# Gates 2 to 5 of an input projection with three of four weight chunks in halves

## The chip, the cores and the metric

The kernel runs on one core of a Trainium2 chip. The metric is the device time of one execution in microseconds. The engines are named as in the profile: PE is TensorE, ACT is ScalarE, DVE is VectorE, POOL is GpSimd, SP is SyncE, which issues the transfers.

## The reference, cut to what matters

Two blocks of two layers each work on 256 tokens of width 1024, in float32. The change lies in the first block, in the mixer of each of its two layers:

```python
h = rmsnorm(x, norm_mix[l])
(u_ssm, q_lat, kv_lat, k_rope, hg_q, hg_f, hg_i, hg_g, gate_logits) = jnp.split(h @ w_in[l], split_at, axis=-1)
...
gates = jax.nn.sigmoid(gate_logits.astype(jnp.float32)).reshape(bsz, s, N_BRANCH, D_MODEL)
merged = (gates[:, :, 0] * y_ssm + gates[:, :, 1] * y_mla + gates[:, :, 2] * y_hg)
x = x + merged @ w_out[l]
```

`gate_logits` is h (256 x 1024) times 3072 columns of `w_in`. The kernel makes it in six products of 512 columns, called gates 0 to 5 here. Between them stands work of the third branch (`hgrn2_mixer`): its attention with decay is built of eight nested levels (distances 64, 32, ... 1, and across the two halves), each of which needs differences and exponentials of summed logarithms, two products by q and k, and small matrix products.

## The kernel before

**Two ways to multiply.** `product` (lines 395 to 402) multiplies float32 operands directly (line 398), or operands that were split into a high and a low half in the type fp32r (line 400): high by high, high by low, low by high, three matmuls. The first is whole, the second in halves. The low half of a value is the value less its high half.

**A gate.** `token_out(("gate", l, n), ...)` runs `token_steps` (line 408): 1024 rows of weights come in four chunks of 256 rows by 512 columns (0.5 MB). Activations are the stationary operand. Of the four chunks the first and the third are whole (`low=None`), the second and fourth are in halves (`halves=mix_half`) and marked "both". The halves of the matching column tiles 2, 3, 6 and 7 of h lie in HTL, made once in each layer by POOL (`halves_of`, line 1345, called in line 1378).

**Buffers and order.** Raw chunks go round four slots of W (`RSLOTS`), the halves of weights round three slots of WH and WL (`HSLOTS`). SP issues the loads in the order of chunks, each when its slot is free: a whole chunk's slot when PE has used it, a split chunk's slot when its low half is made (`chunk_release`). A WH/WL slot is free when PE has used it (`split_release`). A "both" chunk is split by POOL alone (`both_parts`, line 1322). For the marks "dve" and "pool", ACT makes the high half (`split_to`, line 1459, the copy is recorded under line 1450) and DVE or POOL the low half (`low_parts`, line 1152). Each engine does its share in its own instruction order.

**When ACT splits.** Each eviction on ACT goes through `full` (line 1474), which first makes every high half up to `ahead(name)` (line 272): up to two splits after the ones of that bank, as long as their raw chunks lie within four of it. So the splits come before the eviction in ACT's queue. Before the change gates hold no ACT splits.

**The order around it.** PE (lines 802 to 812): wait for `mix_halves`, gate 0, gate 1, level 0, gate 2, levels 1 and 2, gate 3, levels 3 and 4, gate 4, levels 5 and 6, gate 5, level 7. In layer 0 `ssm_out(l, 3)`, which makes y(l,3), stands between gates 0 and 1, in layer 1 ahead of gate 0. It reads `bu[1]`, which is a view of OT. POOL (lines 1378 to 1382): halves of column tiles, the splits up to gate 5, halves of UT, the splits of the next product. ACT (lines 1792 to 1805): gate 0, a logarithm, gate 1, and for n = 2 to 5 the exponentials of levels 2n−3 and 2n−2 and then gate n (a sigmoid); at n = 4 also a gelu. DVE (lines 2480 to 2486): for each level i the difference (line 2432, waits for the exponentials of level i−1), the taking of level i−2 out of its banks (line 2451), and the two products (lines 2444 and 2445, wait for the exponentials of level i), which set `level_ready` for PE; after levels 3 and 5 also some rotary work.

Of the kernel before, what the change touches and what calls it, by code (L numbers as in the profile page):

```python
# [30 lines left out]
KT = DM // P  # L31
# [35 lines left out]
def build(nc, T, out):  # L67

    with ExitStack() as ctx:
# [14 lines left out]
        HTF = nc.alloc_sbuf_tensor_at("HTF", [P, KT, S], F32, offset=ht_at)  # L84
# [112 lines left out]
        mix_half = (HTL[:, 0:4, :], HTL[:, 4:8, :])  # L197
        glu_half = (OTR[:, 0:2, :], OTR[:, 2:4, :])
        half_slot = lambda k: 2 * (k // 4) + k % 2
        oML = OT[:, 4:8, :]  # L200
# [130 lines left out]
        def _(pe):  # L331
# [75 lines left out]

            def token_steps(tag, wname, l, act, K, c0, cols, low="dve", kstep=2, halves=None):

                ps = [begin(*tag, tt) for tt in range(TT)]  # L410
                for k0 in range(0, K, kstep):
                    src, slot = act, lambda k: k
                    if halves and k0 // kstep % 2:
                        n, w = chunk(tag, rows(wname, l, k0, kstep, c0, cols), kstep, cols, "both")
                        src, slot = halves, half_slot
                    else:
                        n, w = chunk(tag, rows(wname, l, k0, kstep, c0, cols), kstep, cols, low)
# [275 lines left out]
            for l in range(DEPTH):  # L693
# [109 lines left out]
                for n in range(2):  # L803
                    if l == 0 and n == 1:
                        ssm_out(l, 3)
                    token_out(("gate", l, n), "w_in", l, HTF, KT, 3360 + 512 * n, 512, low=None, halves=mix_half)
                level(l, 0)
                for n in range(2, 6):
                    token_out(("gate", l, n), "w_in", l, HTF, KT, 3360 + 512 * n, 512, low=None, halves=mix_half)
                    level(l, 2 * n - 3)  # L810
                    if n < 5:
                        level(l, 2 * n - 2)
# [433 lines left out]
        def _(pool):  # L1246
# [97 lines left out]

            def halves_of(dst, src, *ks):


                pair = lambda t, k: t[:, k:k + 2, :].rearrange("p a b -> p (a b)")
                for k in ks:
                    high, low = pair(dst[0], half_slot(k)), pair(dst[1], half_slot(k))  # L1350
                    link(pool.tensor_copy(high, pair(src, k)))
                    ins = pool.tensor_tensor(low, pair(src, k), high.bitcast(F32), ALU.subtract)
                    if k != ks[-1]:
                        link(ins)
                return ins
# [5 lines left out]
            for l in range(DEPTH):  # L1361
# [14 lines left out]


                signal(halves_of(mix_half, HTF, 2, 6), "mix_halves", l + 1)
                split_to(split_before["gate", l, 5, 1])
                pool.wait_ge(sem["y_ready"], 4 * (l + 1))  # L1380
# [1390 lines left out]
```

How the kernel before makes its waits and increments, by code:

```python
        def wait_full(eng, name, split_to=None):  # L281
            b, n = group[name]
            if split_to:
                split_to(ahead(name))
            eng.wait_ge(sem[f"bank_full{b}"], n)
# [4 lines left out]
        def wait_freed(eng, name):  # L292
            b, n = group[name]
            eng.wait_ge(sem[f"bank_free{b}"], n)
# [41 lines left out]
            def begin(*name):  # L337
                while done["n"] % BANKS in unfinished:
                    done["n"] += 1
                b = done["n"] % BANKS
                done["n"] += 1
                use = uses[b] = uses.get(b, 0) + 1
                unfinished.add(b)
                assert name not in group, name
                group[name] = (b, use)
                if use > 1:
                    pe.wait_ge(sem[f"bank_free{b}"], use - 1)
                return banks[b]
# [10 lines left out]
            def chunk(name, srcs, k, cols, low="dve"):  # L359
                n = len(chunks)
                chunks.append((name, srcs, k, cols))
                if low is None:
                    pe.wait_ge(sem[f"w_full{n % RSLOTS}"], raw_full(n))
                    return n, W[:, n % RSLOTS, 0:k * cols].rearrange("p (k n) -> p k n", k=k)
                m = len(splits)
                splits.append((n, low))
                split_of[n] = m
                s, v = low_done(m)
                pe.wait_ge(sem[s], v)
                chunk_release[n] = (s, v)
                return n, [w[:, m % HSLOTS, 0:k * cols].rearrange("p (k n) -> p k n", k=k) for w in (WH, WL)]
```

## Time and profile before

| what | value |
| --- | --- |
| time, median of 3 runs | 1924.55 us (1923.4 to 1927.83) |
| time of the profiled execution | 1924.34 us |
| its span | 1922.6 us |
| PE busy | 1798.9 us, 94% |
| DVE busy | 1220.9 us, 64% |
| ACT busy | 867.1 us, 45% |
| POOL busy | 314.5 us, 16% |
| chain that ended last, PE's share | 81% (line 400: 47%, line 398: 24%) |

The span is the profiled execution from its first to its last instruction; 1.7 us of its time lie outside. The gates of layer 0 stand at 145 to 235 us, those of layer 1 at 753 to 841 us.

### The profile page before, as it was taken

Reading aid. Unit: us, or ns where it says so; the run is one execution under the profiler, and the core shown is the slowest. Engines: PE = TensorE matmul, PEld = TensorE weight load, DVE = VectorE, ACT = ScalarE, POOL = GpSimd, SP = SyncE. Lnnn points to the kernel's source line nnn. Section 1 sums busy time; section 2 is a strip of 40 time slices with the busy share of each in tenths; the row PEclk is TensorE's granted clock in tenths of the full one; section 3 lists DMA queues with packets and bytes.
Section 4 is the critical chain, followed back from the end, with each engine's and each line's share of the span. In section 5 each row is a group of like instructions: output and inputs, shape, how many; then the busy total and the mean of one; then the engine's idle time right before and its main releaser. Section 6 shows DMA issues by size and latency. Waiting matters only on the chain.

```text
span 1922.6 us, 27084 instructions
## 1 busy us (share of the span) xinstructions
PE 1798.9 (94%) x10038; PEld 1442.9 (75%) x10038; DVE 1220.9 (64%) x1879; ACT 867.1 (45%) x1413; POOL 314.5 (16%) x290
## 2 busy tenths in 40 slices
PE   7999988989999999999888999998899999889998
PEld 6676667669998866667478998656799874669987
DVE  8996755445667892855555566565577746546775
ACT  4224445355444412344455445345555543555553
POOL 5015453020000003457012000101200000130000
PEclk9999999999999999999999999999999999899999
DMA  5444442446565444445154656431455644135554
GB/s 160 131 127 151 133 152 88 143 106 185 159 187 180 122 134 132 138 144 170 37 170 138 188 176 197 143 99 66 121 177 164 197 148 126 56 102 173 167 188 138
DMA packets 192359, 274.61 MB, mean 143 GB/s; under 512 B 25616, under 2 KB 129540, under 8 KB 192228
## 3 DMA queue, kind: packets, MB, share of 16 engines
q1 hardware_dynamic: 191364, 269.86, 45.9%
q0 software_dynamic: 864, 3.02, 0.6%
q8 instruction: 80, 1.31, 0.3%
q14 instruction: 51, 0.42, 0.1%
HBM read 271.78 MB, written 1.05 MB: 142 GB/s over the span
## 4 chain that ended last, share of the span: by engine, by line
PE 81%; DVE 8%; ACT 6%; issue 3%; POOL 1%; DMA 1%; DVEq 0%; ACTq 0%; SPq 0%; POOLq 0%
PE bank L400 47%; PE bank L398 24%; DVE WL L1161 2%; ACT WH L1450 2%; PE bank L671 1%; PE bank L585 1%; POOL WL L1161 1%; PE bank L1021 1%; PE bank L593 1%; PE bank L488 1%; PE bank L871 1%; ACT HTH L1450 1%; DVE bank L2108 1%; DVE NMX L2160 0%; PE bank L1041 0%
## 5 line engine op out<-in xcount | busy, mean ns | idle before, releaser
L1161 DVE TENSOR_TENSOR WL<-W,WH 128x1024 fp32r<-128x1024 f32 x288 | 352.9, 1225 | 230.7 <-ACT WH L1450 222.3
L1450 ACT ACTIVATE WH<-W 128x1024 fp32r<-128x1024 f32 x328 | 347.6, 1060 | 314.3 <-PE bank L400 262.4
L400 PE MATMUL bank<-HTH,WH 128*128 128x256 f32 x1536 | 437.6, 285 | 19.6 <-DVE WL L1161 9.5
L400 PE MATMUL bank<-HTL,WH 128*128 128x256 f32 x1536 | 434.6, 283 | 0.0
L400 PE MATMUL bank<-HTH,WL 128*128 128x256 f32 x1536 | 434.5, 283 | 0.0
L400 PEld LDWEIGHTS bank<-HTH,WH 128*128 128x128 f32 x1536 | 294.6, 192 | 25.2 <-DVE WL L1161 11.7
L400 PEld LDWEIGHTS bank<-HTL,WH 128*128 128x128 f32 x1536 | 294.7, 192 | 0.1
L400 PEld LDWEIGHTS bank<-HTH,WL 128*128 128x128 f32 x1536 | 294.6, 192 | 0.0
L400 PE MATMUL bank<-WH,HTL 128*128 128x512 f32 x672 | 262.9, 409 | 0.0
L400 PE MATMUL bank<-WH,HTH 128*128 128x512 f32 x480 | 193.7, 404 | 15.4 <-POOL WL L1161 9.3
L400 PE MATMUL bank<-WL,HTH 128*128 128x512 f32 x480 | 189.6, 395 | 0.0
L398 PE MATMUL bank<-W,M 128*128 128x512 f32 (+1 forms) x416 | 170.7, 568 | 8.6 <-issue 8.6
L400 PEld LDWEIGHTS bank<-WH,HTL 128*128 128x128 f32 x672 | 127.7, 190 | 32.1 <-issue 5.5
L398 PE MATMUL bank<-W,HTF 128*128 128x512 f32 (+1 forms) x384 | 149.8, 539 | 0.0
L398 PEld LDWEIGHTS bank<-W,M 128*128 128x128 f32 x416 | 82.9, 204 | 82.7 <-issue 78.0
L1161 POOL TENSOR_TENSOR WL<-W,WH 128x1024 fp32r<-128x1024 f32 x40 | 96.9, 2423 | 260.5 <-ACT WH L1450 259.6
L1289 POOL TENSOR_SCALAR QSQ<-QSQ 128x2 f32<-128x2 f32 x9 | 5.1, 570 | 754.3 <-ACT PB L1490 754.3
L400 PEld LDWEIGHTS bank<-WH,HTH 128*128 128x128 f32 x480 | 92.0, 192 | 40.8 <-POOL WL L1161 12.4
L398 PEld LDWEIGHTS bank<-W,HTF 128*128 128x128 f32 x384 | 68.2, 190 | 67.5 <-issue 66.1
L400 PEld LDWEIGHTS bank<-WL,HTH 128*128 128x128 f32 x480 | 91.8, 191 | 18.4
L398 PE MATMUL bank<-HTF,W 128*128 128x256 f32 x448 | 99.6, 381 | 0.6 <-DVE HTF L2383 0.6
L1334 POOL TENSOR_TENSOR WL<-W,WH 128x1024 fp32r<-128x1024 f32 x40 | 97.1, 2428 | 3.2
(405 smaller groups left out, 2506.9 us busy)
## 6 DMA issues: line engine op xcount, KB each, us to landing
W<-in_w_in SPq DMA_DIRECT2D x132, 512.0 KB, 3.7
W<-in_ffn_w_gate_up SPq DMA_DIRECT2D x176, 256.0 KB, 3.4
W<-in_w_up SPq DMA_DIRECT2D x176, 256.0 KB, 3.4
W<-in_ffn_w_down SPq DMA_DIRECT2D x44, 512.0 KB, 4.2
W<-in_w_down SPq DMA_DIRECT2D x44, 512.0 KB, 4.2
W<-in_w_out SPq DMA_DIRECT2D x32, 512.0 KB, 4.3
W<-in_ssm_w_glu SPq DMA_DIRECT2D x16, 512.0 KB, 4.3
W<-in_x_w_kv SPq DMA_DIRECT2D x16, 512.0 KB, 3.4
```

The costliest lines, as they stand in the source:

```text
L398: return pe.matmul(out, at_a(a), at_b(b), start=start, stop=stop, skip_group_check=True)
L400: m = pe.matmul(out, at_a(a[x]), at_b(b[y]), start=(start and i == 0), stop=(stop and i == 2), skip_group_check=True)
L488: m = pe.transpose(ps[:, k * S + tt * P:k * S + tt * P + P], X[:, tt, (2 * j + k) * P:(2 * j + k) * P + P], IDENT[:, :])
L585: ins = pe.matmul(ps[:, tt * S:tt * S + S], qT[:, tt * P:tt * P + P], kT, start=(tt == 0), stop=(tt == TT - 1), skip_group_check=True)
L593: ins = pe.transpose(ps[:, kt * S + tt * P:kt * S + tt * P + P], p_buf(tag, m[1])[:, tt, kt * P:kt * P + P], IDENT[:, :])
L671: m = pe.matmul(ps[:, h * P:h * P + P], ka[:, h, b * P:b * P + P], qa[:, h, b * P:b * P + P], start=(h == 0), stop=(h == HGH - 1), skip_gr ...
L871: m = pe.matmul(ps[64 * (h % 2):64 * (h % 2) + 64, 0:S], vtok[:, kt, h * VD:h * VD + VD], PT[h % 2][:, kt, :], start=(kt == 0), stop=(kt = ...
L1021: pe.matmul(ps[:, tt * S:tt * S + S], qkT[r:r + 64, h // 2, tt * P:tt * P + P], qkT[r:r + 64, 4 + h // 4, :], start=(tt == 0), stop=False, ...
L1161: eng.tensor_tensor(WL[:, m % HSLOTS, 0:width], W[:, n % RSLOTS, 0:width], h, ALU.subtract)\
L1334: signal(pool.tensor_tensor(low, raw, high.bitcast(F32), ALU.subtract), s, v)
L1450: copy = lambda dst, src, scale=1.0: act.activation(dst, src, ACT.Copy, scale=scale)
L2108: signal(tt_(g, g, RB, ALU.mult), "g_scaled", FT * aff_no(tag, l) + f + 1)
```

## The change

A second pair of tiles, `mix_half2`, in the last four slots of OTR (a view of OT), takes the halves of column tiles 4 and 5 of h. POOL makes them once in each layer, after the splits of gate 0 and after y(l,3) is complete in its bank, and signals `mix_halves2`. PE waits for that ahead of gate 2. In gates 2 to 5 the third chunk (k0 = 4) is no longer whole: it is marked "pool", so ACT makes the high half of the weights and POOL the low half, and PE multiplies it in halves. Only the first chunk of these gates stays whole. Gates 0 and 1 are as before.

```diff
+        mix_half2 = (OTR[:, 4:6, :], OTR[:, 6:8, :])
...
-            def token_steps(tag, wname, l, act, K, c0, cols, low="dve", kstep=2, halves=None):
+            def token_steps(tag, wname, l, act, K, c0, cols, low="dve", kstep=2, halves=None, halves2=None):
...
+                    elif halves2 and k0 == 4:
+                        n, w = chunk(tag, rows(wname, l, k0, kstep, c0, cols), kstep, cols, "pool")
+                        src, slot = halves2, lambda k: k - 4
...
                 level(l, 0)
+                pe.wait_ge(sem["mix_halves2"], l + 1)
                 for n in range(2, 6):
-                    token_out(("gate", l, n), "w_in", l, HTF, KT, 3360 + 512 * n, 512, low=None, halves=mix_half)
+                    token_out(("gate", l, n), "w_in", l, HTF, KT, 3360 + 512 * n, 512, low=None, halves=mix_half,
+                              halves2=mix_half2)
...
-            def halves_of(dst, src, *ks):
+            def halves_of(dst, src, *ks, slot=half_slot):
...
-                    high, low = pair(dst[0], half_slot(k)), pair(dst[1], half_slot(k))
+                    high, low = pair(dst[0], slot(k)), pair(dst[1], slot(k))
...
                 signal(halves_of(mix_half, HTF, 2, 6), "mix_halves", l + 1)
+                split_to(split_before["gate", l, 0, 1])
+                wait_full(pool, ("y", l, 3))
+                signal(halves_of(mix_half2, HTF, 4, slot=lambda k: k - 4), "mix_halves2", l + 1)
                 split_to(split_before["gate", l, 5, 1])
```

## Rows read from the trace of the kernel before

**Rows 1.** Windows over both layers' gates, sum row: length, busy by engine, means.

```profile
sum 178.25, PE 178.25 PEld 119.85 DVE 122.66 ACT 74.69 POOL 89.09; mean PE 89.12 PEld 59.93 DVE 61.33 ACT 37.34 POOL 44.55
```

**Rows 2.** Chain that ended last, layer 0, 158 to 220 us: start, length, what.

```profile
159.02 3.63 PE bank L398 x8
162.65 2.76 PE bank L400 x12
...
168.84 2.73 PE bank L400 x12
...
185.70 3.57 PE bank L671 x32
...
201.60 3.57 PE bank L671 x32
...
217.51 3.57 PE bank L671 x32
```

**Rows 3.** The same chain in layer 1.

```profile
771.32 3.43 PE bank L398 x8
...
791.60 3.57 PE bank L671 x32
```

**Rows 4.** Timeline of POOL, layer 0: start, length, line, operation, tiles, count, idle before.

```profile
138.31 0.61 POOL L1351 CAST HTL<-HTF 128x512 fp32r<-128x512 f32 x1
139.00 1.26 POOL L1352 TENSOR_TENSOR HTL<-HTF,HTL 128x512 fp32r<-128x512 f32 x1
...
154.26 1.04 POOL L1332 CAST WH<-W 128x1024 fp32r<-128x1024 f32 x1 [1.30 <-DMA W<-in_w_in]
155.38 2.40 POOL L1334 TENSOR_TENSOR WL<-W,WH 128x1024 fp32r<-128x1024 f32 x1
...
176.13 2.72 POOL L1334 TENSOR_TENSOR WL<-W,WH 128x1024 fp32r<-128x1024 f32 x1
```

**Rows 5.** Timeline of POOL, layer 1, first split of gate 1.

```profile
761.59 1.04 POOL L1332 CAST WH<-W 128x1024 fp32r<-128x1024 f32 x1 [2.74 <-issue]
```

**Rows 6.** Timeline of ACT, layer 0, gate 1 and level 1.

```profile
170.30 1.28 ACT L1551 ACT_TABLE_LOAD   x1 [8.69 <-PE bank L400]
171.59 1.23 ACT L1551 ACTIVATE A<-bank 128x512 f32<-128x512 f32 x2
173.01 1.28 ACT L1780 ACT_TABLE_LOAD   x1 [0.20 <-DVE TB L2432]
174.31 0.63 ACT L1780 ACTIVATE TB<-TB 128x512 f32<-128x512 f32 x1
```

**Rows 7.** Groups of instructions by form, ACT: the high halves of weights.

```profile
L1450 ACT ACTIVATE WH<-W 128x1024 fp32r<-128x1024 f32 x328 | 347.6, 1060 | 314.3 <-PE bank L400 262.4 <-DMA W<-in_w_out 30.3 <-issue 14.3
```

**Rows 8.** Loads of line 1237 at 150 to 180 us, from issue to landing.

```profile
DMA to landing us min/median/max: 3.7/4.3/5.6
```

**Rows 9.** Timeline of DVE, layer 0: products of levels 1, 2, 4 and 6.

```profile
176.63 2.77 DVE L2445 TENSOR_TENSOR TB<-TB,HK 128x512 f32<-128x512 f32 x1
...
183.56 2.77 DVE L2445 TENSOR_TENSOR TB<-TB,HK 128x512 f32<-128x512 f32 x1
...
201.97 0.69 DVE L2445 TENSOR_TENSOR TB<-TB,HK 128x512 f32<-128x512 f32 x1
...
215.19 2.66 DVE L2444 TENSOR_TENSOR TB<-TB,HQ 128x512 f32<-128x512 f32 x1
217.88 0.69 DVE L2445 TENSOR_TENSOR TB<-TB,HK 128x512 f32<-128x512 f32 x1
```

**Rows 10.** Windows around longer idle times of PE: stretch, busy, PEclk, DMA.

```profile
416.40:421.30 4.90, 2.10 (x8) 1.05 (x7) 0.00 (x0) 2.08 (x2) 4.74 (x2) 1.00 0.26 68
...
1290.50:1293.50 3.00, 0.06 (x1) 0.00 (x0) 0.00 (x0) 2.25 (x4) 1.15 (x1) 0.88 0.02 7
1293.50:1296.00 2.50, 2.46 (x6) 2.05 (x7) 1.71 (x8) 1.73 (x3) 1.20 (x1) 0.50 0.00 0
1296.00:1300.00 4.00, 4.00 (x12) 3.18 (x11) 3.12 (x12) 1.07 (x4) 0.00 (x0) 0.55 0.00 0
```

## The prediction

> **What bounds the kernel now.** I read the windows first, then the chain of work that ended last, and then the timelines of POOL, ACT and DVE over the same stretch. The change touches gates 0 to 5 of the two layers. There PE is busy for the whole length of both stretches, 178.25 of 178.25 us [rows 1], so a PE microsecond taken out shortens the run, as long as nothing else is late by then. Per gate the chain shows four chunks and two levels: from level 1 to level 3 it is 201.60 − 185.70 = 15.90 us [rows 2]. A chunk in halves (12 matmuls, line 400) takes 2.73 to 2.76 us, a whole one (8 records, line 398) 3.43 us [rows 2, 3].
>
> Second, how late could the others be? The levels wait for `level_ready`, which ends a chain that DVE and ACT pass to each other: difference, exponentials, two products, next difference. Level 2 is ready at 183.56 + 2.77 = 186.33 and PE wants it at 185.70 + 1.78 = 187.48: 1.15 us to spare. Level 4: 202.66 against 203.38. Level 6: 218.57 against 219.29 [rows 2, 9]. So in layer 0 three levels have 0.7 to 1.15 us of cover. The tables call PE the bound, but this chain runs at nearly its pace.
>
> **Removed.** Four gates in two layers: 8 chunks go from 3.43 to 2.73 us, 0.70 each: −5.6 us, all of it in PE's gap-free stretches. If nothing else moved, 1924.34 − 5.6 = 1918.7.
>
> **Added: the halves of two column tiles, in POOL's queue.** A copy of 0.61 and a subtraction of 1.26 us of 128x512, about 2.0 with gaps [rows 4]. They stand between gate 0's splits and gate 1's, behind a wait for y(l,3). Queued behind them are gate 1's two "both" splits, on which PE waits.
> In layer 0 y(0,3) is made by PE after gate 0 and ends at 159.02, where gate 1 begins [rows 2]. Before, POOL split gate 1's first "both" chunk at 154.26 to 157.78 [rows 4], under gate 0. Now the earliest is 159.2 (wait) + 2.0 + 1.04 + 2.40 + gaps 0.2 = 164.8, and PE wants it at 162.65 [rows 2]: a stall of 2.15 us that nothing covers. It is at least that by the code; with a slow subtraction (DVE works on UT in the same moment; POOL's 1024-wide one goes from 2.40 to 2.72 when DVE interferes [rows 4]) perhaps 3.
> In layer 1 y(1,3) comes before gate 0, and POOL has 2.74 us of idle time ahead of its split at 761.59 [rows 5]. The 2.0 us fit in: nothing. If that cover were gone, POOL would still be done with it well before PE asks at 768.58.
> PE's own new wait for `mix_halves2` before gate 2 costs nothing: it is set some 10 us earlier.
>
> **Added: ScalarE's high half, 8 times 1.06 us [rows 7].** Its place matters more than its length. ACT makes the splits that come up to two after gate n before it takes gate n out of its bank. For gate 1 that is gate 2's third chunk. Its raw slot is free only when PE is done with gate 1's third chunk, which is whole, and a load takes 3.7 to 5.6 us to land, 4.3 in the median [rows 8]. Queued behind that wait on ACT are gate 1's two evictions and the exponentials of level 1, on which DVE and then PE's level 1 and 2 wait.
> Layer 0, hand replay: PE ends gate 1's third chunk at 168.84 + 2.1 = 170.9 [rows 2]; landed 175.1; high done 176.15; table load and evictions 1.28 + 1.23, table load and exponentials 1.28 + 1.29 [rows 6], so level 1's exponentials end at 181.3 instead of 175.6: 5.7 us later, while PE is 2.1 us later.
> For later gates the slot is freed by POOL's split, so the load comes early and ACT's extra 1.06 us lies in its idle time: nothing.
>
> **Added: POOL's low half, 8 times 2.40 us, and what it does to DVE.** POOL's own load is no problem: per gate 2 × 3.5 + 2.4 = 9.4 us of work (with the casts) in 15.2. The price is on DVE. Its product of line 2445 takes 0.69 us at 201.97 [rows 9] but 2.77 at 176.63, where POOL's subtraction ran from 176.13 to 178.85 [rows 4]: DVE ended 0.55 us after POOL. Line 2444 shows it at 215.19 with 2.66. From level 4 ready to level 6 ready [rows 9] is 218.57 − 202.66 = 15.91 us, of which this block is 1.97: unhindered about 13.9. PE's new period is 15.90 − 0.70 = 15.2. So the chain keeps up if POOL blocks it for at most 15.2 − 13.9 = 1.3 us a gate, and there are now three POOL subtractions a gate instead of two.
> The Trainium skill (SBUF — State Buffer, "Who interferes with whom") calls this a lock: a DVE instruction with two inputs in SBUF and a GpSimd instruction that reads SBUF exclude one another for the whole instruction, whichever came first. By that rule, the trace agrees (2.77 us against 0.69), and it speaks against the change: read alone, it would block one more DVE step per gate.
>
> Carrying the replay on in layer 0 with POOL at DMA pace: POOL subtracts at 179.8 to 182.1, and level 1 is ready at about 183.4; the next split's subtraction (185.5 to 188.1) holds the product, so level 2 is ready at 189.4. PE wants it at 185.70 + 2.15 − 0.70 + 1.78 = 188.9: stall 0.5. Levels 4 and 6 come out at 204.9 against 204.6 and 220.4 against 220.1: 0.3 each. PE's stall moves POOL's next load too, so the two stay coupled. Together 1.1 us.
> In layer 1 the third chunk of gate 1 ends at 774.75 [rows 3]; landed 779.0, exponentials of level 1 done about 785.2; level 2 ready at about 793.1 against 791.60 + 1.78 − 0.70 = 792.7 [rows 3]: stall 0.4, and levels 4 and 6 just in time.
> The two bounds: no stall of levels at all (0 us), and one more blocked DVE step of 2 us a gate that PE pays in levels 2, 4 and 6 of both layers (12 us, less the slack; see the rival). I take 1.5, from the replay, as its steps are all durations of rows.
>
> **The sum.** −5.6 + 2.15 + 1.1 + 0.4 = −1.95 us. Against the profiled execution's own 1924.34 (span 1922.6) that is 1922.4; the median, 1924.55, is 0.2 above that execution, so the measured median may come 0.2 higher. Behind the gates the code is the same, and the chain there hangs on PE's last glu chunks, so a shift is passed on.
>
> **Rivals.**
> *The level chain is never late.* If POOL's subtractions fall into DVE's waits for ACT, only the stall at gate 1 of layer 0 stands: −5.6 + 2.15 = −3.45, 1920.9. For it: DVE waits for ACT in each level. Against it: ACT's late start of level 1 in layer 0. Chance 0.22.
> *Everything is hidden,* the stall at gate 1 too: 1918.7. It needs POOL to split before y(0,3), which its order forbids: 0.04.
> *DVE and ACT become the bound (slower).* One mechanism: POOL's third subtraction blocks a chain step for another 2.0 us (2.66 − 0.69) in each gate. Then the chain takes 13.9 + 2 × 2.0 = 17.9 against PE's 15.2, 2.7 us for levels 4 and 6 in two layers, 10.8, with 1.5 for level 2: −3.45 + 10.8 = 7.4 or more, 1931.7; half of it, one extra block in every second gate, is 1927 to 1928. It decides from 1.3 us of blocking a gate on. For it: thin slack [rows 2, 9]. Against: POOL's times follow PE's, so a late PE moves POOL's operations later as well, and a blocked step catches up in the waits. Chance 0.17 in all, of which 0.12 above 1928.
> *The clock falls at the new stall.* After 3.0 us without PE work at 1290.5 the granted clock was 0.50 and then 0.55 over 6.5 us (1.2 instead of 2.4 GHz for 6.1 of them), about 3 us lost; during 2.4 us stalls at 416 to 421 it stayed at 1.00 [rows 10]. A stall of 2.15 is like the second. If it falls, 1922.4 + 3 = 1925.4. Chance 0.07.
>
> **How the numbers follow.** Forecast 1922.4, with 0.50 for that case (1921.5 to 1924, the rest of its spread from DMA landing 3.7 to 5.6 us). The range reaches down to 1919.5, which holds the second case with the scatter of runs, and up to 1927.5, which holds the clock case and a milder DVE bound; what is left out is the strong DVE bound and the fully hidden case, under 0.2. A measurement of this kernel can tell about 0.2%, 3.85 us: faster means below 1920.7, which the case of 1920.9 and the hidden one reach about half the time and the forecast seldom: 0.2. Slower means above 1928.4: 0.14. Within: 0.66.
>
> **What would show it.** Line 400 with 96 more matmuls of 128x512 and line 398 with 64 fewer records; PE idle by about 2 us near 162.7 to 164.8, waiting for POOL's WL (line 1334), and none near 768; ACT's sigmoid load for gate 1 at about 176 and 780 instead of 170.3 and 776.2, behind a WH copy of line 1450; short PE waits for DVE (line 2445) ahead of levels 2, 4 and 6; DVE's products of 2.7 us more often. The prediction is wrong if there is no stall at gate 1, or if the stalls ahead of the levels add up to more than 3 us.

## The result and the profile after

The changed kernel takes 1935.82 us in the median of 7 runs (1930.62 to 1937.38), the kernel before 1924.55 beside it: a ratio of 1.0054, 95% interval [1.0042, 1.0066], so 8 to 13 us slower. Ratios here and below are estimated from the single executions of both kernels, and so differ a little from the quotient of two medians; one execution of the kernel before, beside runs 13 to 16, took 3015.54 us at a mean granted clock of 0.554 and is left out of every comparison. The forecast was 1922.4, with 1927.5 as its upper end. The profiled execution took 1936.56 us, its span is 1934.5 (before: 1922.6).

The page of the changed kernel, busy times of its first part, and the shares by engine of the chain that ended last:

```profile
PE 1802.3 (93%) x10070; PEld 1454.5 (75%) x10070; DVE 1238.0 (64%) x1879; ACT 875.5 (45%) x1421; POOL 345.3 (18%) x302
...
PE 75%; DVE 11%; ACT 6%; issue 3%; POOL 2%; DMA 1%; SPq 1%; DVEq 0%; ACTq 0%; POOLq 0%
```

POOL has 30.8 us more. Its twelve new instructions account for 22.9 of them (8 subtractions of 2.40, 2 times 0.61 + 1.26); the other 7.9 us are instructions that take longer than before. DVE has the same 1879 instructions as before and is busy 17 us longer: nobody gave it work, so it was held. And PE's share of the chain fell from 81% to 75%.

The windows over the gates (layer 0 from its first whole chunk behind y(0,2) on, layer 1 as a whole; length, busy and count of PE, PEld, DVE, ACT, POOL, granted clock, DMA share, GB/s):

```profile
152.68:242.98 90.30, 83.01 (x381) 60.32 (x381) 69.26 (x81) 39.85 (x49) 58.61 (x32) 0.98 0.42 136
759.98:853.22 93.24, 87.65 (x385) 64.28 (x386) 62.92 (x75) 38.35 (x48) 58.89 (x33) 0.98 0.42 141
```

PE was never idle there before [rows 1]. Now it is idle for 7.3 and 5.6 us. The timeline of PE in both stretches, all pieces with idle time ahead of them (start, length, line, operation, tiles, count, idle before and its releaser):

```profile
165.60 0.50 PE L401 MATMUL bank<-WH,HTL 128*128 128x512 f32 x1 [2.10 <-POOL WL L1342]
192.98 2.05 PE L677 MATMUL bank<-TB 128*128 128x128 f32 x16 [3.02 <-DVE TB L2456]
210.62 2.83 PE L677 MATMUL bank<-TB 128*128 128x128 f32 x16 [2.17 <-DVE TB L2456]
...
802.57 3.49 PE L677 MATMUL bank<-TB 128*128 128x128 f32 x16 [2.51 <-DVE TB L2456]
837.75 2.05 PE L677 MATMUL bank<-TB 128*128 128x128 f32 x16 [3.08 <-DVE TB L2456]
```

The first is the stall at gate 1, forecast with 2.15 us. The other four stand ahead of levels, 10.8 us together, where the forecast had 1.5. All wait for `level_ready`, DVE's second product (line 2456, 2445 before). The account, by place: against before, the work at the start of layer 0's gates comes 0.85 us later (the chunk at 152.68 stood at 151.83), the chunk behind level 7 in layer 0 7.8 us later (242.98 against 235.20), in layer 1 the start 7.4 and the end 12.1 us later, the end of the run 11.9. So the loss arises in the gates and at their start: −5.6 saved, +12.9 idle, +0.85 at the start, −0.6 between and behind the gates, and by difference from 11.9 another 4.4 us in which PE works but slowly, which is looked at below. The 0.85 us at the start lie within the scatter of executions: kernels 2, 3, 5, 8 and 11 below have the same code up to that point and the same stall of 2.10 us there, and it ends between 163.34 and 165.20 us, in the changed kernel at 165.60.

Why DVE is late shows in the timelines of POOL and DVE ahead of level 2:

```profile
187.26 2.37 POOL L1342 TENSOR_TENSOR WL<-W,WH 128x1024 fp32r<-128x1024 f32 x1
189.71 2.67 POOL L1169 TENSOR_TENSOR WL<-W,WH 128x1024 fp32r<-128x1024 f32 x1
192.45 1.38 POOL L1340 CAST WH<-W 128x1024 fp32r<-128x1024 f32 x1
193.90 3.22 POOL L1342 TENSOR_TENSOR WL<-W,WH 128x1024 fp32r<-128x1024 f32 x1
...
203.76 1.04 POOL L1340 CAST WH<-W 128x1024 fp32r<-128x1024 f32 x1 [6.63 <-DMA W<-in_w_in]
```

```profile
187.88 2.30 DVE L2455 TENSOR_TENSOR TB<-TB,HQ 128x512 f32<-128x512 f32 x1
190.21 2.71 DVE L2456 TENSOR_TENSOR TB<-TB,HK 128x512 f32<-128x512 f32 x1
192.96 1.94 DVE L2443 TENSOR_TENSOR TB<-TB 128x1024 f32<-128x1024 f32 x1
```

The three subtractions of a gate run back to back, with one cast between them, 187.26 to 197.12, and then POOL waits 6.63 us for its next load. DVE's first product ends 0.55 us behind the first subtraction, the second 0.54 us behind the second one, and the difference 1.07 us behind the cast; unhindered each product takes 0.69 us, the difference 1.23. Three DVE steps in a row are held, 1.61 + 2.02 + 0.71 = 4.3 us. Level 2 is ready at 192.92 and level 4, by the same pattern, at 210.57: 17.65 us, where PE's new period is 15.2.

### The profile page after: what moved, and what is told of

It is laid out like the page before. It is cut to its first block, busy times and chain, and to the rows that moved or that the text cites. A ratio compares the mean times of both kernels' runs of the same rounds, so it can differ in the third digit from the quotient of the medians.

```text
span 1934.5 us, 27188 instructions
## 1 busy us (share of the span) xinstructions
PE 1802.3 (93%) x10070; PEld 1454.5 (75%) x10070; DVE 1238.0 (64%) x1879; ACT 875.5 (45%) x1421; POOL 345.3 (18%) x302
## 3 DMA queue, kind: packets, MB, share of 16 engines
q0 software_dynamic: 864, 3.02, 0.5%
HBM read 271.78 MB, written 1.05 MB: 141 GB/s over the span
## 4 chain that ended last, share of the span: by engine, by line
PE 75%; DVE 11%; ACT 6%; issue 3%; POOL 2%; DMA 1%; SPq 1%; DVEq 0%; ACTq 0%; POOLq 0%
PE bank L401 45%; PE bank L399 21%; DVE WL L1169 2%; ACT WH L1461 2%; PE bank L591 1%; POOL WL L1169 1%; PE bank L599 1%; PE bank L1029 1%; DVE TB L2456 1%; DVE TB L2455 1%; PE bank L879 1%; DVE TB L2443 1%; ACT HTH L1461 1%; PE bank L494 1%; PE bank L677 1%
## 5 line engine op out<-in xcount | busy, mean ns | idle before, releaser
L1461 ACT ACTIVATE WH<-W 128x1024 fp32r<-128x1024 f32 x336 | 356.0, 1059 | 339.5 <-PE bank L401 264.6
L401 PEld LDWEIGHTS bank<-HTH,WH 128*128 128x128 f32 x1536 | 294.5, 192 | 24.9 <-DVE WL L1169 11.5
L401 PE MATMUL bank<-WH,HTL 128*128 128x512 f32 x672 | 258.7, 402 | 2.1 <-POOL WL L1342 2.1
L1169 POOL TENSOR_TENSOR WL<-W,WH 128x1024 fp32r<-128x1024 f32 x48 | 116.9, 2435 | 272.7 <-ACT WH L1461 264.3
L399 PE MATMUL bank<-W,HTF 128*128 128x512 f32 (+1 forms) x320 | 121.9, 531 | 0.0
L1342 POOL TENSOR_TENSOR WL<-W,WH 128x1024 fp32r<-128x1024 f32 x40 | 100.1, 2504 | 3.2
L399 PEld LDWEIGHTS bank<-W,HTF 128*128 128x128 f32 x320 | 56.5, 192 | 56.0 <-issue 55.1
```

The source lines that it names most:

```text
L399: return pe.matmul(out, at_a(a), at_b(b), start=start, stop=stop, skip_group_check=True)
L401: m = pe.matmul(out, at_a(a[x]), at_b(b[y]), start=(start and i == 0), stop=(stop and i == 2), skip_group_check=True)
L1169: eng.tensor_tensor(WL[:, m % HSLOTS, 0:width], W[:, n % RSLOTS, 0:width], h, ALU.subtract)\
L1342: signal(pool.tensor_tensor(low, raw, high.bitcast(F32), ALU.subtract), s, v)
L1461: copy = lambda dst, src, scale=1.0: act.activation(dst, src, ACT.Copy, scale=scale)
```

## The experiments

The kernel before ran beside each, with medians of 1924.97 (1 to 4), 1925.52 (5 to 8), 1926.04 (9 to 12) and 1926.02 us (13 to 16). "Idle" is PE's idle time in the gates of both layers, from the timeline of the profiled execution.

**1. The stall at gate 1 alone.**

```diff
-                split_to(split_before["gate", l, 0, 1])
+                split_to(split_before["gate", l, 1, 1])
                 wait_full(pool, ("y", l, 3))
                 signal(halves_of(mix_half2, HTF, 4, ...), "mix_halves2", l + 1)
```

> The changed kernel, with POOL making the halves of tiles 4 and 5 after gate 1's splits instead of before them. Theory (three causes: POOL's order at gate 1, ACT's wait for a landing, DVE held by POOL's subtractions): PE's 2.10 us idle at gate 1 of layer 0 disappears, none of the others do; layer 0's gates shorten by about 2.1 us, layer 1's stay, 1934.5 for the median (after: 1935.8 to 1936.6). Rival (PE's stall only moves the slack, the level chain sets the end of the gates): POOL's splits no longer queue up, but ACT still starts level 1 late and the idle ahead of level 2 grows by 2 us, time as after, 1936.

Measured: 1934.5 us, ratio 1.0039 [1.0024, 1.0054]. The stall at gate 1 is gone, the idle time ahead of levels is 11.5 us (2.72, 2.27, 2.92, 0.55, 3.04). The median is 1.3 us below the changed kernel's and the idle time 1.4 us: a small point, which the scatter alone could hide; the large one is elsewhere.

**2. ScalarE's high half behind level 1.** In front of gate 1's evictions ACT no longer makes splits ahead; gate 2's high half comes after the exponentials of level 1.

```diff
-                gate(1)
+                for tt in range(TT):
+                    wait_full(act, ("gate", l, 1, tt))
+                    free_after(act.activation(gates[:, tt, 512:1024], ...), "gate", l, 1, tt)
...
                     level_exps(2 * n - 3)
+                    if n == 2:
+                        split_to(ahead(("gate", l, 1, 0)))
```

> The changed kernel, with ACT taking gate 1 out of its bank and making level 1's exponentials before it makes gate 2's high half, in both layers. Theory: the chain DVE-ACT starts 4 to 6 us earlier, the idle ahead of level 2 (3.02 and 2.51 us) goes, the ones ahead of levels 4 and 6 stay or move; 1936 − 5 = 1931. Rival (POOL's subtractions alone set the pace of the level chain): the idle ahead of level 2 goes, but each gate of levels then takes over 17 us against 15.2, so 2 us come back at level 4 and again at level 6, and the time falls by less than 2 us.

Measured: 1938.92 us, ratio 1.0063 [1.0048, 1.0078]. PE's timeline in layer 0:

```profile
163.48 0.50 PE L401 MATMUL bank<-WH,HTL 128*128 128x512 f32 x1 [2.10 <-POOL WL L1342]
181.04 0.50 PE L401 MATMUL bank<-WH,OTR 128*128 128x512 f32 x1 [0.43 <-POOL WL L1169]
185.47 0.50 PE L401 MATMUL bank<-WH,HTL 128*128 128x512 f32 x1 [1.42 <-POOL WL L1342]
208.50 2.05 PE L677 MATMUL bank<-TB 128*128 128x128 f32 x16 [3.05 <-DVE TB L2461]
224.56 2.05 PE L677 MATMUL bank<-TB 128*128 128x128 f32 x16 [0.58 <-DVE TB L2461]
```

The 3.02 us ahead of level 2 are gone, so ACT's late start of level 1 was behind them. But POOL's low half now waits for ACT (its idle time of 7.84 us ended with `WH`), all splits behind it are late, and the stalls come back as PE's wait for WL and at level 4, 13.3 us in all. The rival's picture is the nearer one, a stall that comes back at level 4; the gain of 5 us that the theory forecast is absent. Repairing one link lengthened another.

**3. Most of the third subtraction taken away.** The low half is made for 16 of 1024 columns; those of the other columns aren't made, and PE multiplies what an earlier chunk left there.

```diff
         def low_parts(eng, who, done, upto):
...
+                    if chunks[n][0][0] == "gate":
+                        width = 16
```

> The changed kernel, but POOL's low half of the third chunk of gates 2 to 5 is made for 16 of 1024 columns only: the rest of that low half is left over from an earlier chunk, so this part of the computation is left out. Theory (DVE held by POOL's third subtraction): DVE's two products no longer both take 2.3 to 2.8 us, a gate of levels takes 16 us or less, PE's idle ahead of levels 4 and 6 goes, and the time falls from 1936 to about 1929. Rival (ACT's wait for the landing is the cause): the idle ahead of level 2 stays at 2.5 to 3 us and the time falls by under 2 us.

Measured: 1925.48 us, ratio 1.0000 [0.9988, 1.0012], 10 us less than the change, with ACT's high half, its wait and the stall of 2.10 us all still there. Idle 3.6 us: 2.10 at gate 1, 0.76 and 0.77 ahead of one level in each layer. DVE is busy 1221.4 us, as before the change. So the loss against before hangs on POOL's third subtraction.

**4. The subtraction alone, in the kernel before.** One subtraction of 128x1024 on POOL between the two splits of each of gates 2 to 5, into a tile that nobody reads then; PE's, ACT's and the queues' work is that of the kernel before.

```diff
-                split_to(split_before["gate", l, 5, 1])
+                split_to(split_before["gate", l, 1, 1])
+                wait_full(pool, ("y", l, 3))
+                for n in range(2, 6):
+                    split_to(split_before["gate", l, n - 1, 1] + 1)
+                    link(pool.tensor_tensor(OTR[:, 4:8, :], HTF[:, 0:4, :], HTF[:, 4:8, :], ALU.subtract))
+                    split_to(split_before["gate", l, n, 1])
```

> The kernel before, with one more POOL subtraction of 128x1024 from SBUF to SBUF between the two splits of each of gates 2 to 5 (its result is not used). No chunk changes, ACT waits for nothing new. Theory (POOL's subtractions hold DVE): DVE's products of 2.3 us and more become as frequent as after, the level chain takes over 16 us a gate, PE idles 1 to 3 us ahead of levels 2, 4 or 6, and the time rises by 3 to 8 us over before. Rival (only ACT's late start does harm): PE stays without idle time and the time is that of before.

Measured: 1935.0 us, ratio 1.0050 [1.0034, 1.0066]; DVE is busy 16 us longer with no work of its own added. POOL and DVE of this kernel in layer 0:

```profile
201.32 2.38 POOL L1334 TENSOR_TENSOR WL<-W,WH 128x1024 fp32r<-128x1024 f32 x1
203.78 2.68 POOL L1383 TENSOR_TENSOR OTR<-HTF 128x1024 fp32r<-128x1024 f32 x1
```

```profile
201.94 2.31 DVE L2449 TENSOR_TENSOR TB<-TB,HQ 128x512 f32<-128x512 f32 x1
204.28 2.72 DVE L2450 TENSOR_TENSOR TB<-TB,HK 128x512 f32<-128x512 f32 x1
207.03 1.94 DVE L2437 TENSOR_TENSOR TB<-TB 128x1024 f32<-128x1024 f32 x1
```

The same picture as in the changed kernel, to 0.01 us in the held products. PE is idle twice, 2.50 and 2.35 us, both ahead of a level; behind the second the level took 3.58 instead of 1.78 us, at a lower granted clock (0.76 over 815 to 822 us). Eight instructions of 2.4 us on an engine that is 16% busy cost 9.6 us. Together with the third run this shows the cause from both sides. How it costs that, and whether another order avoids it, is the question of the others.

**5 to 7. PE asks for the levels later.** If only the deadlines are too early, a later place for the levels gives the chain time.

```diff
                 for n in range(2, 6):
                     token_out(("gate", l, n), ...)
+                    if n > 2:
+                        level(l, 2 * n - 4)
                     level(l, 2 * n - 3)
-                    if n < 5:
-                        level(l, 2 * n - 2)
```

The changed kernel with this edit:

> The changed kernel, with PE doing level 1 after gate 2, levels 2 and 3 after gate 3, 4 and 5 after gate 4, 6 and 7 after gate 5: levels 2, 4 and 6 are asked for a gate (about 13 us) later. Same operations, same POOL subtractions. Theory (PE loses time only because levels 2, 4 and 6 are due before DVE, held by POOL, has them): PE's idle ahead of the levels goes, only the 2.10 us at gate 1 of layer 0 stay, time 1924.5 − 5.6 + 2.1 = 1921 or, if the chain eats up its 13 us, a few us more. Rival (the level chain is slower than the gates for good, 17 us against 15.2, and its end sets the end of the gates wherever PE takes the levels): the idle moves to levels 6 and 7 or to what follows, time 1930 or more.

with the edit of the first run too:

> Both edits: levels later on PE, and POOL's halves of tiles 4 and 5 after gate 1's splits. Theory: PE without idle time in both layers' gates, the full 5.6 us, 1919 against 1925. Rival (POOL's splits then come too late elsewhere, or the glu waits for DVE's last level): about 1921 or more.

and the kernel before with it, as a control:

> Control: the kernel before with the levels later on PE. PE has no idle time in its gates, so theory and rival both expect the time of before, 1924.5 to 1925, if the move itself costs nothing; a faster or slower time would have to be taken off the two runs with the same move.

Measured: 1939.74 us, ratio 1.0072 [1.0057, 1.0087]; 1933.82, ratio 1.0044 [1.0028, 1.0060]; the control 1926.92, ratio 1.0010 [0.9999, 1.0021]. With the control's 0.0010 taken off, that leaves 1.0062 and 1.0034, beside 1.0054 and 1.0039 without the move: no gain. The idle time (12.5 and 10.6 us) stands in more and smaller pieces. A chain that is slower than PE in every gate is not helped by one more gate's time. And a new link closed: ACT's high half stands behind exponentials that wait for DVE, and POOL waits for it. ACT in the fifth kernel:

```profile
204.45 1.06 ACT L1461 ACTIVATE WH<-W 128x1024 fp32r<-128x1024 f32 x1 [9.25 <-DVE TB L2443]
```

**8. The low half by DVE.**

```diff
-                        n, w = chunk(tag, rows(...), kstep, cols, "pool")
+                        n, w = chunk(tag, rows(...), kstep, cols, "dve")
```

> The changed kernel with the low half of the third chunk made by DVE (1.23 us each) instead of POOL (2.40 us each). POOL then subtracts twice a gate as before the change, DVE has 1.23 us more a gate in the level chain. Theory (each POOL subtraction that meets DVE costs it about 2 us): the chain is 0.8 us or more a gate shorter than in the changed kernel, time 1930 to 1934. Rival (the amount of work is what counts, not who does it): DVE is busier than before by 10 us in all, the chain is longer, time 1936 or more.

Measured: 1946.45 us, ratio 1.0115 [1.0096, 1.0134], idle 18.1 us: the rival. DVE needs only 1.23 us for what takes POOL 2.4, but these stand in the chain itself, and some are held in turn:

```profile
208.17 1.94 DVE L2443 TENSOR_TENSOR TB<-TB 128x1024 f32<-128x1024 f32 x1
210.14 3.25 DVE L1169 TENSOR_TENSOR WL<-W,WH 128x1024 fp32r<-128x1024 f32 x1
```

**9 and 10. POOL's subtractions in the gates in four pieces of 256 columns,** so that DVE gets in between.

```diff
...
+                step = width // 4 if chunks[n][0][0] == "gate" else width
+                for c0 in range(0, width, step):
+                    ins = pool.tensor_tensor(low[:, c0:c0 + step], raw[:, c0:c0 + step],
+                                             high.bitcast(F32)[:, c0:c0 + step], ALU.subtract)
...
```

> The changed kernel, with each of POOL's subtractions for the gates' weights (the two of the both chunks and the one of the third chunk) made in four pieces of 256 columns, one after the other, instead of one of 1024. Same elements. Theory (DVE is held for a whole POOL instruction, up to 2.4 us): DVE is let in after a piece of about 0.6 us, its products take at most 1.4 us, DVE's busy time falls from 1238 to 1225 or less, the level chain is back under 16 us a gate, time 1924 to 1928. Rival (the two share the port, and what counts is the amount that POOL moves): DVE's busy time stays near 1238 and the time at 1934 or more.

and with the edit of the first run:

> The same, with POOL's halves of tiles 4 and 5 after gate 1's splits. Theory: the 2.10 us idle at gate 1 of layer 0 goes as well, 1922 to 1926, and if the chain keeps up with 15.2 us a gate, 1919 to 1921, faster than before. Rival: 1932 or more, as in the runs without pieces.

Measured: 1934.61 us, ratio 1.0055 [1.0041, 1.0070], and 1932.28, ratio 1.0041 [1.0025, 1.0056], idle 9.2 and 8.0 us. DVE is let in: the products take 0.69 to 1.22 us and DVE is busy 1225.0 us instead of 1238.0. But POOL's groups by form (busy us, mean ns of one, idle before) and then its timeline show the price:

```profile
L1355 POOL TENSOR_TENSOR WL<-W,WH 128x256 fp32r<-128x256 f32 x96 | 86.8, 905 | 7.6
```

```profile
187.33 4.72 POOL L1355 TENSOR_TENSOR WL<-W,WH 128x256 fp32r<-128x256 f32 x4
192.12 3.46 POOL L1176 TENSOR_TENSOR WL<-W,WH 128x256 fp32r<-128x256 f32 x4
```

A chunk now takes 3.1 to 4.9 us instead of 2.4, PE waits for WL (2.89, 0.87 and 0.75 us in kernel 9), and every small step of DVE may meet a piece:

```profile
197.21 0.78 DVE L2498 TENSOR_TENSOR SCR<-M,RC 128x128 f32<-128x128 f32 x1
```

(0.29 us otherwise). The time stayed. What one engine was spared, the other paid.

**11. POOL does both halves of the third chunk, ACT nothing new** (`"pool"` becomes `"both"`).

> The changed kernel with the third chunk split by POOL alone (cast 1.04 and subtraction 2.40 us), so ACT has nothing new to do and does not wait for a load ahead of gate 1's evictions. Theory: level 1 starts 5 us earlier in layer 0 and 4 us in layer 1, but POOL's subtractions are as many, so each gate of levels still takes 17 us or more: the idle ahead of level 2 shrinks, those ahead of levels 4 and 6 stay, time 1930 to 1934. Rival (ACT's late start is the larger part): all idle ahead of levels goes, 1922.

Measured: 1945.22 us, ratio 1.0100 [1.0086, 1.0114]. The idle time ahead of level 2 shrinks to 0.83 us in layer 0 and 1.28 in layer 1, which confirms ACT's part in it, but 5.36 and 5.35 us stand ahead of level 4, and 16.0 us in all. POOL's timeline there is one block, from the cast at 184.37 to the subtraction that ends at 196.51. POOL has eight casts more here, so this run alone doesn't weigh ACT's part; the third does, which keeps ACT's high half and its wait and loses nothing.

**12. The third chunk in halves only in gate 5,** behind whose levels 5 and 6 nothing but level 7 follows, with the edit of the first run.

```diff
-                              halves2=mix_half2)
+                              halves2=mix_half2 if n == 5 else None)
```

> The changed kernel with POOL's halves after gate 1's splits and only gate 5's third chunk in halves; gates 2 to 4 as before the change. Levels 7 and 8 have 8 us and more to spare. Theory: PE without idle time, 2 times 0.70 us saved, 1923 to 1924, no difference that can be measured from before. Rival (any third POOL subtraction costs 1 us or more, wherever it is): 1926 or more.

Measured: 1924.48 us, ratio 0.9995 [0.9985, 1.0005]; PE is busy for all of the gates. The window of layer 0:

```profile
150.00:240.00 90.00, 90.00 (x393) 61.15 (x392) 63.61 (x82) 37.82 (x48) 50.98 (x30) 1.00 0.44 145
```

Two chunks give 1.4 us by the sum, which this measurement can't tell from nothing.

**13, 14 and 16. POOL's subtractions placed in DVE's waits.** All with the edit of the first run. After a difference, DVE has only the takes out of a bank and the wait for the exponentials to do. In 13 the third chunk's subtraction waits for the difference of level 2n − 3, in 14 the last chunk's also for that of level 2n − 2, and 16 is 14 with gate 2's third chunk left whole. Shown is the edit of 14; 13 has no `pace`.

```diff
+                    if m in pace:
+                        pool.wait_ge(sem["level_diff"], pace[m])
                     signal(pool.tensor_tensor(low, raw, high.bitcast(F32), ALU.subtract), s, v)
...
+                for n in range(2, 6):
+                    pace[split_before["gate", l, n, 1] - 1] = 8 * l + 2 * n - 2
+                    split_to(split_before["gate", l, n, 1] - 2)
+                    pool.wait_ge(sem["level_diff"], 8 * l + 2 * n - 3)
+                    split_to(split_before["gate", l, n, 1] - 1)
```

> The changed kernel with the halves of tiles 4 and 5 behind gate 1's splits, and with one more wait on POOL: the subtraction of gate n's third chunk starts only when DVE has made the difference of level 2n-3, that is, when DVE's next steps are the takes out of a bank and the wait for ScalarE's exponentials. Nothing is left out. Theory (the loss is DVE's products held by the third subtraction, which comes back to back with another one): the two products of levels 2, 4 and 6 are no longer both held, the chain from level 2 to level 4 falls from 17.65 us to 16 or less, idle time of PE ahead of the levels 1 to 3 us in all, time 1921 to 1923, some 12 below the same kernel without the wait (1934.5). Rival (the chain DVE, ACT, POOL is too long in any order): the wait delays POOL's next splits, PE waits for POOL's WL instead, 1930 or more.

> As the kernel before this in the list, and the subtraction of gate n's last chunk (its cast not) also starts only with DVE's difference of level 2n-2. Nothing is left out. Theory: two of the three subtractions of a gate lie in DVE's waits for the exponentials, one falls as it may: at most one held product a gate, as in the kernel before the change, whose chain took 15.9 us a gate; PE's period is 15.2, so 0 to 0.7 us of idle time a level pair, time 1920 to 1922.5. Price if the placing is too tight: by the durations of the rows the second subtraction ends 10.1 us after the even level is ready and PE wants it at 10.7, so any delay shows as PE waiting for POOL's WL of line 1342. Rival: that wait is what is seen, 1928 or more.

> As the second kernel of the list, but gate 2 keeps its whole third chunk: three chunks in halves only in gates 3, 4 and 5, so that 6 chunks are shortened by 0.70 us, 4.2 us in all. ScalarE's high half no longer waits for its load in front of gate 1's evictions. Nothing is left out. Theory: level 1 comes as early as in the kernel before the change, the slack of 0.7 to 1.2 us ahead of levels 2 and 4 is back, and the time is 1921 to 1922, 3 to 4 us below the kernel before. Rival (the chain has no room for a third subtraction in any gate): idle time ahead of levels 4 and 6 of 2 us each in both layers, 1927 or more.

Measured: 1935.45 us, ratio 1.0054 [1.0034, 1.0074]; 1935.78, ratio 1.0049 [1.0032, 1.0066]; 1934.15, ratio 1.0035 [1.0020, 1.0051]. The theories, 1920 to 1923 us by a better order, fell in all three. In 13 idle time is 10.9 us, still ahead of levels: the third subtraction falls where it should (188.32), but the two others meet DVE instead. POOL and DVE of kernel 13:

```profile
191.86 2.72 POOL L1345 TENSOR_TENSOR WL<-W,WH 128x1024 fp32r<-128x1024 f32 x1
...
199.00 2.41 POOL L1345 TENSOR_TENSOR WL<-W,WH 128x1024 fp32r<-128x1024 f32 x1
```

```profile
192.36 2.77 DVE L2463 TENSOR_TENSOR TB<-TB,HK 128x512 f32<-128x512 f32 x1
...
199.19 2.37 DVE L2493 COPY M<-M 128x256 f32<-128x256 f32 x1
```

In 14 the products are held less (1.4 us each), but a subtraction that isn't placed now holds the difference:

```profile
185.02 3.28 DVE L2451 TENSOR_TENSOR TB<-TB 128x1024 f32<-128x1024 f32 x1
```

And it is the rival's picture: PE waits for WL six times, 11.6 us in all, as in layer 0:

```profile
183.05 0.50 PE L401 MATMUL bank<-WH,HTL 128*128 128x512 f32 x1 [2.77 <-POOL WL L1345]
200.54 0.50 PE L401 MATMUL bank<-WH,HTL 128*128 128x512 f32 x1 [2.02 <-POOL WL L1345]
218.02 0.50 PE L401 MATMUL bank<-WH,HTL 128*128 128x512 f32 x1 [1.96 <-POOL WL L1345]
```

One gate takes 17.49 us there (DVE's difference of an odd level starts at 185.02 and at 202.51), against 17.65 in the changed kernel. In 16 the idle time is 9.3 us, again PE's wait for WL (3.75 and 0.91 us in layer 0, 3.71 and 0.93 in layer 1) and not ahead of levels, where its rival had it. Ahead of the first of these POOL sat idle for 7.99 us until DVE's difference was made, by the added wait itself. So 14 and 16 show that this placing is too tight; they don't show that no other has room.

**15. Both known causes away:** the edits of the first and the third run.

> The changed kernel with the halves of tiles 4 and 5 behind gate 1's splits and, in the gates' third chunks, POOL's low half made for 16 of 1024 columns (what is left out: the low halves of the other columns are not made). Theory: with both causes taken away, the stall of 2.10 us at gate 1 and the third subtraction, PE is idle under 1 us in the gates and the time is 1925.5 - 2.1 = 1923.4 or less; by the sum it could be as low as 1919.5. Rival (something else of the change costs time, ScalarE's high half or the late level 1): 1925 or more, with the place of it in the rows.

Measured: 1923.73 us, ratio 0.9990 [0.9979, 1.0000], idle 1.5 us (0.72 and 0.77 ahead of one level in each layer). By the sum, −5.6 + 1.5 = −4.1 us; measured are −1.9, with an interval of −4.0 to 0. The traces say where the difference goes. From gate 1 to the end of level 7 layer 0 takes 82.17 us (153.56 to 235.73) against 83.37 before, layer 1 87.39 (754.60 to 841.99) against 88.53: 2.3 us less in all, which agrees with the measurement. Level 4 is ready 15.60 us after level 2 and level 6 16.19 us after level 4 (188.43, 204.03, 220.22), where PE's period would be 15.2: with only two long subtractions a gate the chain is still slower than the shortened gates, and idle time, short waits and slow restarts take more than half of the saving. This is the best that was measured, 0.1%, and it leaves work out.

All runs in one view; idle and busy times are those of the profiled execution, which can lie some us beside the median:

| kernel | ratio | idle in the gates, us | DVE busy | POOL busy |
| --- | --- | --- | --- | --- |
| changed kernel | 1.0054 | 12.9 | 1238.0 | 345.3 |
| 1 halves late | 1.0039 | 11.5 | 1234.7 | 345.5 |
| 2 ACT late | 1.0063 | 13.3 | 1244.7 | 347.0 |
| 5 levels later | 1.0072 | 12.5 | 1239.1 | 343.6 |
| 6 levels later, halves late | 1.0044 | 10.6 | 1238.8 | 344.6 |
| 8 low half by DVE | 1.0115 | 18.1 | 1233.9 | 320.4 |
| 9 pieces | 1.0055 | 9.2 | 1225.0 | 371.7 |
| 10 pieces, halves late | 1.0041 | 8.0 | 1224.3 | 372.3 |
| 11 both halves by POOL | 1.0100 | 16.0 | 1248.2 | 355.4 |
| 13 third one placed | 1.0054 | 10.9 | 1231.0 | 338.3 |
| 14 two placed | 1.0049 | 11.6 | 1223.3 | 337.7 |
| 16 two placed, gates 3 to 5 | 1.0035 | 9.3 | 1220.7 | 333.0 |
| 4 before, one more subtraction | 1.0050 | 4.9 | 1237.0 | 343.3 |
| 7 before, levels later | 1.0010 | 0.8 | 1230.1 | 313.6 |
| 3 narrow | 1.0000 | 3.6 | 1221.4 | 322.1 |
| 15 narrow, halves late | 0.9990 | 1.5 | 1217.3 | 322.1 |
| 12 gate 5 only | 0.9995 | 0 | 1222.3 | 324.3 |

None of the orders that keep the third subtraction in three or four gates is below 1.0035. An estimate by rows says why this may be more than bad luck: per gate DVE's steps with two operands in SBUF are four products of 0.69, two differences of 1.23 and the twelve small rotary operations (six of 0.29, six of 0.17), 8.0 us; three subtractions of 2.35 on POOL are 7.1. If they exclude one another, that is 15.1 of PE's 15.2 us (before: 12.7 of 15.9), while DVE also has to wait for the exponentials and POOL for loads. The estimate is worked out from durations, not measured; that a better order than those tried doesn't exist isn't shown.

## Why the prediction was wrong, point by point

**The saving** of 0.70 us a chunk held: three halved chunks in a row take 8.2 us in the chain, 2.73 each.

```profile
213.45 4.33 PE bank L399 x8
217.77 8.21 PE bank L401 x36
```

**The stall at gate 1** was right in place, releaser and size (2.10 for 2.15; it lies 0.85 us later than forecast, with all that stands from 151.83 on, see the account above), and so was its absence in layer 1.

**ScalarE's wait** was right: the high half stands at 176.60 in front of the table load and the evictions, the exponentials of level 1 end at 182.80, forecast 181.3; 0.85 of the 1.5 us is the later start.

```profile
176.60 1.06 ACT L1461 ACTIVATE WH<-W 128x1024 fp32r<-128x1024 f32 x1 [14.14 <-DMA W<-in_w_in]
177.67 1.28 ACT L1562 ACT_TABLE_LOAD   x1
```

**The failing step is the replay of the levels,** the term 1.1 + 0.4 = 1.5 us. It let POOL work "at DMA pace", one subtraction here and one there, and so found one held product a gate and, in layer 0, stalls of 0.5, 0.3 and 0.3 us ahead of levels 2, 4 and 6, in layer 1 0.4, 0 and 0. Measured are 3.02, 2.17 and 0 in layer 0, 2.51, 0 and 3.08 in layer 1: 10.8 us, more than the 3 us that the prediction itself had named as the sign of being wrong. What the replay lacked: from 188 us on no load was under way (the DMA share is 0.00 over 188 to 190), so the raw chunks of gate 3 were all there, and from 187.26 on POOL ran gate 3's subtractions in one block, while DVE's two products and the difference were held one after another. The rule for such a chain is in the rows of before themselves: a product ends 0.55 us after the subtraction that holds it [rows 4, 9]. As soon as a second subtraction is queued, the next product starts inside it again. I carried the position of one subtraction per gate and took the others for harmless.

**The budget was misread too.** The 13.9 us of the unhindered chain is 15.91 less one held product, 1.97 us. But the same stretch has a second one, 0.68 us longer than its 0.69, and the stretch ahead of it has two. DVE in the kernel before:

```profile
190.34 1.91 DVE L2444 TENSOR_TENSOR TB<-TB,HQ 128x512 f32<-128x512 f32 x1 [1.22 <-ACT TB L1781]
...
199.38 2.55 DVE L2444 TENSOR_TENSOR TB<-TB,HQ 128x512 f32<-128x512 f32 x1
...
206.68 1.37 DVE L2444 TENSOR_TENSOR TB<-TB,HQ 128x512 f32<-128x512 f32 x1 [1.22 <-ACT TB L1781]
```

With every step's excess over its unhindered time (0.69, 1.23, 0.29 or 0.17 us) taken off, the chain of one gate has nearly the same length in all six stretches looked at:

| stretch | length, us | held | rest |
| --- | --- | --- | --- |
| before, layer 0, level 2 to 4 | 16.33 | 3.08 | 13.25 |
| before, layer 0, level 4 to 6 | 15.91 | 2.65 | 13.26 |
| changed, layer 0, level 2 to 4 | 17.65 | 4.36 | 13.29 |
| changed, layer 1, level 4 to 6 | 18.62 | 5.41 | 13.21 |
| 13, layer 0, level 2 to 4 | 18.87 | 5.67 | 13.20 |
| 15, layer 0, level 2 to 4 | 15.60 | 2.32 | 13.28 |

So the chain bears 15.2 − 13.25 = 1.95 us of holding a gate, not 1.3, and the two subtractions of the kernel before already held it for 2.65 and 3.08: with that placing PE's new period was out of reach before a third one came. The third took the holding to 4.36. In layer 1, ahead of level 6, the 5.41 us are a held difference (3.26 us), a copy and two smaller steps; its two products before the stall were not held.

The bound of "one more blocked step" was there as the slower rival, worked out to 1931.7 or more, and it is the one that came true: its chain of 17.9 us a gate was measured at 17.65. It had 0.17; what it lacked is the 4.4 us of slow work behind the stalls. The argument against it, that POOL's operations move along with a late PE, is what the fifth, thirteenth and fourteenth run contradict: POOL moves, but into other steps of DVE or so late that PE waits for WL.

**What else was held.** The scans of layer 0 and the rotary steps stood in no sum of mine. The scans take 11.32 us against 5.66 before, in the changed kernel with POOL's halves and gate 1's splits beside them:

```profile
162.56 11.32 DVE L2432 TENSOR_TENSOR_SCAN TB<-ONES,TB 128x128 f32<-128x128 f32 x8 [0.85 <-ACT TB L1805]
...
831.08 2.37 DVE L2486 COPY M<-M 128x256 f32<-128x256 f32 x1
```

The scans cost nothing, since level 1 waited for ACT's exponentials until 182.80 anyway. The copy of 2.37 us (0.29 in layer 0) and its neighbours stand ahead of level 6 in layer 1, where the 3.08 us stall is.

**The clock.** I let it stay at a stall of 2.15 us and gave its fall 0.07. It stayed at the 2.10 us stall of gate 1, yet fell at the stalls ahead of level 4 in layer 0 and level 2 in layer 1. Windows behind the idle times:

```profile
193.00:196.00 3.00, 3.00 (x19) 2.44 (x20) 2.93 (x3) 1.03 (x1) 2.92 (x2) 1.00 0.00 0
...
211.00:214.00 3.00, 3.00 (x16) 2.58 (x16) 2.93 (x3) 1.38 (x2) 2.92 (x2) 0.62 0.00 0
214.00:218.00 4.00, 4.00 (x10) 1.91 (x9) 2.62 (x7) 1.16 (x2) 0.76 (x1) 0.86 0.01 2
...
802.50:806.00 3.50, 3.43 (x17) 3.43 (x18) 3.40 (x4) 1.44 (x2) 3.42 (x2) 0.55 0.02 5
```

After 2.17 and 2.51 us without matmuls it was 0.62 and 0.55, near the lower of its two levels (1.2 instead of 2.4 GHz). The first 16 matmuls of a level took 2.83 and 3.49 us instead of 1.78, the whole chunk behind the first 4.33 instead of 3.44. With the slow restarts at the other stalls (2.05 for 1.78, twice, and 3.02 for 2.76) that is 1.05 + 1.71 + 0.89 + 0.54 + 0.26 = 4.45 us, what the account above leaves. All of it stands directly behind stalls; it comes with them and is no cause beside them.

The lock rule of the Trainium skill (SBUF — State Buffer, "Who interferes with whom") was weighed in the prediction as speaking against the change, and taken for one held step. The trace agrees with it step by step: first product 2.30 and second 2.71 us beside subtractions, difference 1.94 us beside a cast, against 0.69, 0.69 and 1.23.

## What to carry to other kernels

Before an instruction is given to the idle one of two engines that exclude one another, take from the trace how long the other engine's chain is without any holding, how much it is held already, and what the bound engine's new period leaves. Here that was 13.25, 2.65 to 3.08, and 15.2 us: the room was used up before the change, though the tables call POOL 16% busy. When a chain is replayed, let the other engine run whatever it can as one block, and give a chain with 1 us of cover the chance of its bound, not of its average. A saving on the bound engine is worth what the second longest chain leaves of it, and a stall can cost more than its length: here 12.9 us of idle time brought 4.4 us of slow work with them.

## What the runs showed of the hardware

- Eight subtractions on POOL, 19 us of its time, on which nobody waits, cost 9.6 us in the kernel before (run 4).
- The hold goes both ways: POOL's subtraction takes 3.22 us when DVE's difference came first (193.90), and a cast, with one input, 1.38 to 1.92 instead of 1.04. Not only products are held: scans (11.32 us for 5.66), a plain copy (2.37 for 0.29).
- A subtraction of 256 columns on POOL takes 0.82 to 0.91 us in the mean (0.72 at the least), one of 1024 columns 2.4: four pieces cost 3.3 to 3.6 us (run 9).
- Executions of one kernel differ with the mean granted clock over the span: of kernel 13, one had 1929.1 us at 0.981 (the profiled one, whose span therefore lies below its median) and one 1940.5 us at 0.976.
- Of five idle times of PE between 2.10 and 3.08 us, the clock fell after two (2.17, 2.51) and not after the longest ones (3.02, 3.08). Other runs have both outcomes too: after 2.12 us (run 9) the clock was 0.72, after 3.40 us (run 13, layer 0) 0.70, after 3.36 us (run 13, layer 1) 1.00. What decides isn't settled by these runs.
